# Spreading the token-mixing tiles of a hybrid decoder layer as 4, 6 and 6 over the projection and two finishing passes

## What is computed

```python
h = rms_norm(x, norm_mix_g[i])
z = h @ w_cols
zs = token_shift(z[..., :RWKV_COLS], mu_shift[i])      # r, k, v, decay, a, gate
y = rwkv7_scan(rh, decay, kh, vh, kk, a)               # sequential in tokens
swa_out = swa_sink_attention(zq, zk, zvv, sinks[i], rel_bias)
x = x + concatenate([rwkv_out, swa_out]) @ w_out[i]
u = rms_norm(x, norm_mlp_g[i])
x = x + square(relu(u @ w_ff_up[i])) @ w_ff_down[i]
e = rms_norm(p[i] @ ple_proj[i], ple_norm_g[i])
x = x + e * sigmoid(x @ ple_gate[i])
return rms_norm(x, final_norm_g)
```

## Time and profile before

| | us |
|---|---|
| median of 3 runs | 2715.58 |
| span of the profiled execution, first to last instruction | 2710.3 |
| median less span | 5.3 |
| PE (TensorE) busy | 2670.7 (99%) |
| DVE (VectorE) busy | 1761.8 (65%) |
| ACT (ScalarE) busy | 1098.8 (41%) |

### The profile page before, as it was taken

One profiled execution on the slowest core, in us unless ns is written; L12 is line 12 of the kernel. 1 busy time (PEld: TensorE's weight loads), 2 busy tenths in 40 slices (PEclk: granted clock), 3 DMA queues, 4 the chain that ended last, 5 costly groups with the idle time before them and its releaser, 6 DMA issues.

```text
span 2710.3 us, 57626 instructions
## 1 busy us (share of the span) xinstructions
PE 2670.7 (99%) x25202; PEld 2164.3 (80%) x25202; DVE 1761.8 (65%) x3037; ACT 1098.8 (41%) x1862; POOL 0.2 (0%) x4
## 2 busy tenths in 40 slices
PE   8999999999999999999999999999999999999998
PEld 6877787787878878878788888787878888888876
DVE  5477887857767674776776756867767565344435
ACT  4354444345333433653344325543434254233225
POOL 0000000000000000000000000000000000000000
PEclk9999999999999999999999999999999999999999
DMA  6564544463333334342332334433332244333332
GB/s 198 152 175 137 154 133 123 130 209 95 93 95 115 90 103 130 132 134 83 109 110 87 107 102 145 149 91 107 94 96 83 90 136 156 101 97 98 93 101 78
DMA packets 376199, 319.16 MB, mean 118 GB/s; under 512 B 48747, under 2 KB 328460, under 8 KB 375948
## 3 DMA queue, kind: packets, MB, share of 16 engines
q1 hardware_dynamic: 372272, 312.63, 38.4%
q10 hardware_dynamic: 3676, 2.84, 0.4%
HBM read 277.65 MB, written 38.14 MB: 117 GB/s over the span
## 4 chain that ended last, share of the span: by engine, by line
PE 79%; ACT 1%; DVE 1%; issue 0%; ACTq 0%
PE ps L818 14%; PE ps L821 13%; PE ps L822 13%; PE ps L860 9%; PE ps L864 9%; PE ps L863 9%; PE ps L703 2%; PE ps L675 1%; PE ps L831 1%; PE ps L774 1%; PE ps L622 1%; PE ps L591 1%; PE ps L614 1%; PE ps L595 1%; PE ps L594 1%; PE ps L628 1%
## 5 line engine op out<-in xcount | busy, mean ns | idle before, releaser
L1292 DVE TENSOR_TENSOR w_lo<-wraw_f,w_hi 128x1024 fp32r<-128x1024 f32 x408 | 497.5, 1219 | 345.8 <-ACT w_hi L980 344.5
L980 ACT ACTIVATE w_hi<-wraw_f 128x1024 fp32r<-128x1024 f32 x408 | 430.2, 1054 | 593.2 <-PE ps L818 504.6
L818 PE MATMUL ps<-w_hi,h_hi 128*128 128x512 f32 x1280 | 509.4, 398 | 3.1 <-DVE act_lo L1645 3.1
L821 PE MATMUL ps<-w_lo,h_hi 128*128 128x512 f32 x1280 | 499.1, 390 | 0.0
L822 PE MATMUL ps<-w_hi,h_lo 128*128 128x512 f32 x1280 | 499.0, 390 | 0.0
L860 PE MATMUL ps<-act_hi,w_hi 128*128 128x512 f32 x1024 | 412.6, 403 | 1.5 <-DVE w_lo L1292 1.4
L864 PE MATMUL ps<-act_hi,w_lo 128*128 128x512 f32 x1024 | 399.4, 390 | 0.0
L863 PE MATMUL ps<-act_lo,w_hi 128*128 128x512 f32 x1024 | 399.3, 390 | 0.0
L1172 ACT ACTIVATE h_hi<-tmp 128x512 fp32r<-128x512 f32 x128 | 80.9, 632 | 511.3 <-DVE tmp L1636 511.3
L818 PEld LDWEIGHTS ps<-w_hi,h_hi 128*128 128x128 f32 x1280 | 240.2, 188 | 58.1 <-issue 8.8
L822 PEld LDWEIGHTS ps<-w_hi,h_lo 128*128 128x128 f32 x1280 | 240.3, 188 | 51.7
(11 more groups left out here) (227 smaller groups left out, 3731.1 us busy)
## 6 DMA issues: line engine op xcount, KB each, us to landing
wraw_f<-in_w_ff_up SPq DMA_DIRECT2D x256, 256.0 KB, 3.3
wraw_f<-in_w_ff_down SPq DMA_DIRECT2D x128, 512.0 KB, 4.0
wraw_f<-in_w_in SPq DMA_DIRECT2D x80, 512.0 KB, 4.4
zT<-tmp SPq DMA_DIRECT2D x80, 256.0 KB, 2.1
wraw_f<-in_w_out SPq DMA_DIRECT2D x32, 512.0 KB, 4.2
wraw_f<-in_w_gate SPq DMA_DIRECT2D x32, 512.0 KB, 3.9
zs<-zT SPq DMA_DIRECT2D x16, 896.0 KB, 5.8
h_lo<-mixT SPq DMA_DIRECT2D x4, 2048.0 KB, 8.8
```

The costliest lines, as they stand in the source:

```text
L818: mm = T.matmul(ps[:, j, :], ah, wh, start=(first and k == 0), stop=False)
L821: T.matmul(ps[:, j, :], ah, wl, start=False, stop=False)
L980: S.activation(w_hi[:, n % 2, :], raw[:, n % 4, :], ACT.Copy).then_inc(w_hi_done, 1)
L1292: V.tensor_tensor(w_lo[:, n % 2, :], raw[:, n % 4, :], w_hi[:, n % 2, :].bitcast(F32), ALU.subtract).then_inc(w_lo_done, 1)
```

## The change

The 12 tiles that were mixed beside the first, second and third finish (four to each) are mixed beside the first and the second (six to each). The list of places for a finish has 156 entries in place of 104, and the third and the fourth finish run alone. The list for the projection is as before.

```diff
--- before.py
+++ after.py
@@ -184,10 +184,12 @@
                43, 44, 44, 45, 46, 47, 48, 49, 51, 52, 53, 54, 55, 56, 57, 58, 59, 61, 61, 63, 65, 65, 66, 66, 68, 68, 72, 72, 74,
                75, 77, 78, 79, 80, 81, 82, 83, 84, 84, 85, 85, 86, 87, 88, 88, 90, 91, 91, 92, 92, 93, 95, 97, 97, 98, 99, 101, 103,
                104, 105, 107, 108, 109, 110, 110, 111, 111, 112, 113, 115, 117, 118, 119)
-BESIDE_FIN = (0, 2, 2, 3, 3, 6, 6, 8, 11, 13, 19, 23, 25, 27, 29, 30, 32, 33, 34, 35, 36, 37, 39, 39, 41, 41, 42, 42, 42, 46, 46,
-               47, 47, 48, 49, 50, 52, 53, 55, 57, 59, 60, 62, 63, 64, 65, 66, 67, 69, 70, 71, 71, 72, 73, 73, 73, 78, 78, 78, 79,
-               80, 82, 84, 85, 87, 89, 91, 93, 95, 96, 97, 98, 100, 101, 104, 104, 105, 105, 106, 106, 106, 110, 110, 111, 112, 112,
-               113, 115, 116, 119, 121, 123, 127, 129, 132, 133, 134, 137, 138, 143, 146, 148, 149, 154)
+BESIDE_FIN = (0, 1, 1, 3, 3, 5, 6, 7, 8, 10, 11, 12, 13, 14, 15, 16, 17, 18, 19, 19, 20, 21, 23, 23, 25, 26, 26, 27, 27, 29, 30, 32,
+               32, 33, 34, 36, 37, 38, 39, 41, 42, 43, 44, 44, 45, 46, 46, 48, 49, 49, 51, 52, 53, 54, 54, 55, 56, 58, 59, 60, 61,
+               62, 64, 65, 66, 67, 68, 69, 70, 70, 71, 72, 73, 74, 75, 76, 77, 79, 79, 80, 80, 82, 82, 84, 85, 86, 87, 89, 90, 91,
+               92, 93, 94, 95, 96, 97, 98, 98, 99, 100, 102, 102, 104, 105, 105, 106, 106, 108, 109, 111, 111, 112, 113, 115, 116,
+               117, 118, 120, 121, 122, 123, 123, 124, 125, 125, 127, 128, 128, 130, 131, 132, 133, 133, 134, 135, 137, 138, 139,
+               140, 141, 143, 144, 145, 146, 147, 148, 149, 149, 150, 151, 152, 153, 154, 155, 156, 158)
 
 
 def side_by_side(fill, tiles, places):
@@ -217,10 +219,11 @@
         for _ in part:
             pass
     side_by_side(one_after_another(proj(1), proj(2), proj(3)), [mix(t) for t in range(TPB)], BESIDE_PROJ)
-    for b in range(1, BLOCKS):
-        side_by_side(fin(b - 1), [mix(t) for t in range(b * TPB, (b + 1) * TPB)], BESIDE_FIN)
-    for _ in fin(BLOCKS - 1):
-        pass
+    for b in range(2):
+        side_by_side(fin(b), [mix(t) for t in range(TPB + 6 * b, TPB + 6 * (b + 1))], BESIDE_FIN)
+    for b in range(2, BLOCKS):
+        for _ in fin(b):
+            pass
 
 
 STAGES = {}
```

## The result

| | before | after |
|---|---|---|
| median, us | 2714.72 (2712.09 to 2715.61, 4 runs) | 2856.94 (2854.58 to 2860.31, 4 runs) |
| after / before, 95% interval | | 1.0527 (1.0514 to 1.054) |
| PE busy, us | 2670.7 (99%) | 2712.7 (95%) |
| DVE busy, us | 1761.8 | 1759.3 |
| ACT busy, us | 1098.8 | 1094.4 |

The change makes the kernel slower by 142.2 us. The forecast was 2798, slower by 82, with a range of 2737 to 2845: the direction was right, the size fell outside the range.

A forecast was written before the change was run, and what follows sets the result against it. TensorE, busy 99%, was taken as the bound, its stalls adding one for one. Waits of 21.8 + 8.0 + 6.5 + 4 = 40.3 us per mixed finish, twice, plus 3.4, less some 2, gave +82: 2798 us, range 2737 to 2845.

The forecast's parts named there:

- The mechanism: Up-projections: DVE issues in order, idles 1.22 us for ScalarE's squares before h_lo, so PE waits at the next step.
- fourth tile: Steps 7 to 14, places 86 to 94, group 2's up-projection: PE waits of 0.2 to 2.3 us, 6.6 with lighter steps.
- 18 and 19 at place 98: Two dependent steps sharing a place, where DVE first has relu and h_lo: PE waits 2.5 us.
- last_scale and step 10: Second finish only: step 9 at place 10 comes behind four last_scale of 1285 ns, 3.4 us.
- step 8 at place 140: Its 6.4 us of DVE stand before additions that free the down-projection's banks: PE 3.2 us late.
- point (c) of the rivals: Clock falls to its lower level behind long PE waits: +5 to 7 us; with (b), chance 0.15.
- rival (b): Backlogs add up: ScalarE's delays return as late w_lo in heavy stretches, about 2840; chance 0.15 with (c) on top.
- The turning stretches: Places 16 to 19 and 153 to 156, engines handing over small pieces: 4 us per finish, bounds 0 and 7.5.
- the tiles' own heavy stretches: PE waits following the second to fifth tiles' steps through a mixed finish: 6.2, 6.3, 6.6 and 2.7, together 21.8 us.
- (a): Finishes behave like the projection, PE losing 1 to 1.5 us per tile: about 2730; chance 0.20.
- (d): No change: PE was never late before and its queue absorbs everything, 2713 to 2719; chance 0.07.
- six pairs: Steps with no place between them, the second's matmuls needing the first's result: 8.0 us per mixed finish.

The follow-up runs named there:

- experiment 2: Changed kernel with VectorE's h_lo issued behind the mixing step of its place in up-projections instead of before it: 2820.68 us, 36.3 less.
- experiment 6: Kernel before the change, with h_lo likewise issued behind the mixing step of its place: 2713.55 us against 2713.30, ratio 1.0.
- experiment 4: Kernel before, four tiles per mixed finish, its places replaced by the new list's first 104, stretched evenly over 0 to 154: 2835.13 us, 120.8 more.
- experiment 7: Changed kernel, its 156 places per finish chosen anew from each engine's order and trace durations: 2755.35 us, ratio 1.0155 to the kernel before.
- experiment 8: Changed kernel with h_lo behind the mixing step and places chosen anew for that order: 2735.76 us, ratio 1.0082 to the kernel before.
- experiment 3: Kernel before, with TensorE made to wait for VectorE's relu or h_lo at some chunks of the last, unmixed finish: 2754.47 us, 40.1 more.

## Why the prediction was right in direction and wrong in size

**What held.** The bound: PE's time is the time, and each wait is added to the end one for one. The parts of nothing: no matmul and no DVE instruction more, both lone finishes as forecast (about 455 and 471; 461.1 and 471.6), no PE wait on a transfer in the finishes. The mechanism: DVE in its one order, with the 1.22 us that it can't fill (experiments 2 and 6). The sign that the forecast named for it: L706 in the up-projections at 3.00 in place of 0.77.

**The waits one by one.** In the second mixed finish, start to start less 0.23 of the matmul's own, forecast and measured: fourth tile 1.7, 1.65 and 2.3, 2.3; the second tile's two of 1.9, 1.95 (w_lo) and 1.75 (kappa); 18 and 19 at place 98 2.5, 2.4; 19 and 20 1.0, 0.97; step 14 ahead of out_add 2.2, 2.4; step 24 at 51 0.7, 1.0; last_scale and step 10 3.4, 4.0; only step 8 at place 140 is far off, 3.2 against 1.5. There the prediction's own terms, 6.4 of DVE against 2.0 + 2.7 of PE, give 1.7. So bookkeeping by hand from durations of the trace found where PE is late, and by how much, for these steps.

**The step that failed** is the clock, point (c) of the rivals: "at most three or four waits of over 3 us", "none as long as that one" and "+5 to 7, inside the range", left out of the sum. Each of its parts was too low. Eight waits in the mixed finishes are over 3 us, and two of them, 5.06 and 5.04 from start to start, are longer than the 4.50 of the one in the projection. Intervals of 2.2 to 2.8 us were enough several times. And the 16 stretches at half clock last 5.5 us each, where the one of the earlier trace rows lasts 3.4. Their cost is about 42 us. The only row that I had was of a longer wait. My own sum named six waits of 1.9 to 3.2 us per finish and one of 3.4; what the clock does behind those no row of before told, and so that cost belonged in the sum with two ends, nothing and the price of the earlier trace rows for each.

**Two terms were too small.** Step 0 to 1, the table loads on ACT, in four of five cases behind the squares: 19.5 us by the waits, and not in the sum. I named ScalarE in rival (b), as a backlog, and never followed its order for one tile as I had DVE's. The turning stretches, taken at 4 with bounds 0 and 7.5, measured 8.5 per finish (1.1, 1.4, 3.05 and 2.95). Together these are 19.5 + 2 x 4.5 = 28.5 more. The rest of the sum came out 13 less, 3.4 of that at step 8 of place 140. Most of it must lie in the tiles' own heavy stretches: with the other terms as measured, they come by subtraction to some 32 us, an estimate, where the sum had 2 x 21.8. So the waits are 99 where the sum had 84, and 84 + 15 + 42 = 141. Neither miss alone leaves the range: 2798 + 42 is 2840 and 2798 + 15 is 2813; that it took both is why 2856.94 lies above 2845.

**Rivals.** (a), the projection's pace at 2730, and (d), no change, fell. (b), 2840 by backlogs that add up, came nearest in number and not in cause: of the excess over the forecast 42 us are the clock, and late w_lo, its mechanism, holds PE for 5.2 + 4.1 us in the mixed finishes (L821 and L863), part of which the sum had.

**DVE's share** was forecast near 72% in the mixed finishes and is 465.90 / 673.90 = 69%: the same work in a longer stretch.

**Slips.** The prediction calls the stretch from 1244.2 an up-projection alone and mixed; by their lines (L818, L821, L822) the rows from 1244.2 and 2330.9 in the earlier trace rows are down-projections, and the one from 2374.4 the up-projection. Both take 43.5 us alone and 56 to 57 mixed, so nothing in the sum hangs on it. For the pair at place 98 it writes 2.6 + 0.85 - 1.2 = 2.5; that makes 2.25, and 2.4 was measured. It says six pairs and prices eight, as many as the list has.

**What I hadn't asked** is which of two changes does the harm, for the edit makes both: the distribution, and a list that is even. Experiments 4, 7 and 8 answer: evenness alone costs 121 with four tiles, six tiles with fitted places 42, and 22 with h_lo behind the step as well.

## What to carry over

Where two pieces of work are interleaved in one fixed order, the place of a step counts, not the mean density: follow each engine's order through one tile by hand, ScalarE and its table loads as well as VectorE. A sum of waits of TensorE needs a second line for the clock: ask of each wait, is it long enough to bring the clock down, and price that from a row or an experiment. A wait taken away at one step is worth nothing until one has looked at which step is late next.

## What the runs showed of the hardware that I had not expected

- A TensorE wait of 2.8 us idle (3.17 from start to start) brought the granted clock to 0.50 each of eight times and cost 1.6 us beyond its length; four waits of 0.9 us did not. In the changed kernel intervals of 1.97 to 2.78 us went either way.
- A table load of 1.28 us on ScalarE, hidden in the kernel before but for one wait of 0.3 us, held TensorE once it stood behind work of its own stage: 0.62 us of activations cost a wait of 4.8 us.
- A loss of 142 us moved PE's busy time by only 42 us (2670.7 to 2712.7), about as much as the clock's part; in experiment 3 it is 17 us for 12.5, in experiment 4 43 for 38. The waits show in the share, the clock in the busy time.
